# Two-block transformer kernel: the order of the second block's attention units, and where its selection rounds run

## The reference

```
x = x + hybrid_mixer(rms_norm(x))      # dsa and nsa attention, 8 heads each
x = x + memory_xattn(rms_norm(x), mem)
x = x + sq_relu_mlp(rms_norm(x))
```

```
idx_score = sum over heads of relu(qi . ki) * wi, causal
sel       = top 128 keys of idx_score                      # "dsa"
o_dsa     = softmax(qd . kd over sel) . vd
o_cmp     = masked_softmax(qn . kc) . vc                   # 31 compressed keys
o_slc     = softmax(qn . ks over selected blocks) . vs
o_win     = softmax(qn . kw in a window of 512) . vw
o_nsa     = gate0 * o_cmp + gate1 * o_slc + gate2 * o_win
out       = concat(o_dsa, o_nsa) @ w_out
```

## Time and profile before

| | us |
|---|---|
| time, median of 3 runs | 2523.76 (2520.18 to 2527.74) |
| profiled execution, time | 2526.07 |
| profiled execution, span on the core | 2523.9 |
| PE busy in it | 2429.9 (96%) |
| DVE busy | 1228.2 (49%) |
| ACT busy | 930.3 (37%) |
| POOL busy | 1227.3 (49%) |

### The profile page before, as it was taken

One profiled execution on the slowest core, in us unless ns is written; L12 is line 12 of the kernel. 1 busy time (PEld: TensorE's weight loads), 2 busy tenths in 40 slices (PEclk: granted clock), 3 DMA queues, 4 the chain that ended last, 5 costly groups with the idle time before them and its releaser, 6 DMA issues.

```text
span 2523.9 us, 33202 instructions
## 1 busy us (share of the span) xinstructions
PE 2429.9 (96%) x12413; PEld 1945.3 (77%) x12413; DVE 1228.2 (49%) x2251; ACT 930.3 (37%) x1471; POOL 1227.3 (49%) x1594
## 2 busy tenths in 40 slices
PE   7899999999999999999999999998998998999999
PEld 5778777888888778877788878887665667788887
DVE  6885653452335668356333143255688644511211
ACT  5233442432322532244242232244335755423322
POOL 3444445555556645354555555565333432555554
PEclk9999999999999999999999999999898899999999
DMA  4222322332222232222233223233210011222222
GB/s 158 85 81 72 92 67 91 107 105 99 94 98 92 92 101 79 82 84 72 88 100 125 95 90 100 88 105 109 75 63 18 2 38 39 99 93 100 94 99 92
DMA packets 81294, 218.57 MB, mean 87 GB/s; under 512 B 15856, under 2 KB 25456, under 8 KB 80752
## 3 DMA queue, kind: packets, MB, share of 16 engines
q1 hardware_dynamic: 61920, 200.96, 24.3%
q10 hardware_dynamic: 19216, 15.51, 2.2%
HBM read 207.78 MB, written 2.10 MB: 83 GB/s over the span
## 4 chain that ended last, share of the span: by engine, by line
PE 83%; DVE 11%; ACT 2%; issue 2%; ACTq 1%; POOL 1%; DMA 0%; DVEq 0%
PE psG L1007 25%; PE psG L1009 24%; PE psG L1008 24%; PE psT L1184 2%; PE psS L1163 2%; DVE work_b L2048 1%; PE psO L1217 1%; DVE work_m L2048 1%; DVE tmp L2048 1%; ACTq L1700 1%; DVE work_b L2513 1%; PE psS L1094 1%; DVE max L2512 1%; DVE small_work L2048 1%; PE psG L1163 0%
## 5 line engine op out<-in xcount | busy, mean ns | idle before, releaser
L946 POOL TENSOR_TENSOR w_lo<-w_raw,w_hi 128x256 fp32r<-128x256 f32 (+1 forms) x1482 | 1156.2, 810 | 1188.4 <-ACT w_hi L1569 1188.3
L1007 PE MATMUL psG<-h_hi,w_hi 128*128 128x512 f32 x1880 | 751.1, 400 | 12.4 <-POOL w_lo L946 4.1
L1008 PE MATMUL psG<-h_lo,w_hi 128*128 128x512 f32 x1880 | 737.1, 392 | 0.0
L1009 PE MATMUL psG<-h_hi,w_lo 128*128 128x512 f32 x1880 | 736.8, 392 | 0.0
L1569 ACT ACTIVATE w_hi<-w_raw 128x1024 fp32r<-128x1024 f32 (+4 forms) x417 | 404.0, 969 | 501.1 <-PE psG L1009 485.8
L1007 PEld LDWEIGHTS psG<-h_hi,w_hi 128*128 128x128 f32 x1880 | 356.3, 189 | 103.7 <-issue 18.4
L1009 PEld LDWEIGHTS psG<-h_hi,w_lo 128*128 128x128 f32 x1880 | 355.7, 189 | 75.4
L1008 PEld LDWEIGHTS psG<-h_lo,w_hi 128*128 128x128 f32 x1880 | 356.7, 190 | 73.0 <-issue 1.9
L1007 PE MATMUL psG<-m_hi,w_hi 128*128 128x512 f32 x800 | 311.8, 390 | 1.1 <-DVE m_lo L2048 1.1
L1009 PE MATMUL psG<-m_hi,w_lo 128*128 128x512 f32 x800 | 311.5, 389 | 0.0
L1008 PE MATMUL psG<-m_lo,w_hi 128*128 128x512 f32 x800 | 311.4, 389 | 0.0
(11 more groups left out here) (359 smaller groups left out, 2592.5 us busy)
## 6 DMA issues: line engine op xcount, KB each, us to landing
w_raw<-wstream SPq DMA_DIRECT2D x327, 512.0 KB, 3.3
w_raw<-wstream SPq DMA_DIRECT2D x64, 256.0 KB, 2.6
w_raw<-wstream SPq DMA_DIRECT2D x16, 384.0 KB, 3.0
work_b<-work_b ACTq DMA_DIRECT2D x16, 256.0 KB, 3.8
work_b<-cmpw ACTq DMA_DIRECT2D x2, 2048.0 KB, 8.9
x<-xT SPq DMA_DIRECT2D x4, 512.0 KB, 7.9
small_work<-ssmp ACTq DMA_DIRECT2D x8, 256.0 KB, 2.8
outT<-x SPq DMA_DIRECT2D x8, 256.0 KB, 2.0
```

The source lines that it names most:

```text
L946: ins = pool.tensor_tensor(lo[:, c], w[:, c], hi[:, c].bitcast(F32), ALU.subtract)
L1007: pe.matmul(out, whi, hi, start=(k == 0), stop=False)
L1008: pe.matmul(out, whi, lo, start=False, stop=False)
L1009: ins = pe.matmul(out, wlo, hi, start=False, stop=(k == K - 1))
```

## The change

- `SELECT_EACH` becomes a table by product: three rounds in most waves of K = 8, one in waves of K = 1 or 2, two in some, none in the last two (`("uq", 3)` and `("p2", "qn3")`) nor behind them. 23 of the 48 rounds then run in the projections and 25 beside attention. Since the heads of query block 1 are issued only once round 8 of block 2 is chosen, these heads move three waves down.
- `BLOCK2_ORDER` becomes `BLOCK2_PAIRS`. Units of nsa 3 alternate with those of nsa 0, dsa 3 with dsa 0, nsa 2 with nsa 1, dsa 2 with dsa 1. The two `cmp` units of a pair of lists stand side by side. The two lists of a pair use different output banks, and both outputs come at the end of the pair.
- The waits on compressed probabilities follow the new order.
- After the projections PE runs five matmuls of constants (128x256) whose result nobody reads, once the last product's bank is free.
- ACT computes one dummy Exp ahead of attention's first.

```diff
-SELECT_EACH = 3
+SELECT_EACH = {("p2", "kc"): 2, ("kvd",): 1, ("p2", "vs"): 3, ("kd",): 1, ("p2", "vw"): 3, ("uq", 0): 1, ("p2", "qn0"): 3,
+               ("uq", 1): 1, ("p2", "vc"): 2, ("p2", "qn1"): 3, ("uq", 2): 1, ("p2", "qn2"): 2}
...
-BLOCK2_ORDER = [("nsa", 3), ("dsa", 3), ("nsa", 2), ("nsa", 1), ("nsa", 0), ("dsa", 0), ("dsa", 2), ("dsa", 1)]
+BLOCK2_PAIRS = [(("nsa", 3), ("nsa", 0)), (("dsa", 3), ("dsa", 0)), (("nsa", 2), ("nsa", 1)), (("dsa", 2), ("dsa", 1))]
...
-    for kind, b in BLOCK2_ORDER:
-        lists[kind, b] = (units_nsa if kind == "nsa" else units_dsa)(b)
+    block2 = []
+    for large, small in BLOCK2_PAIRS:
+        for kind, b in (large, small):
+            lists[kind, b] = (units_nsa if kind == "nsa" else units_dsa)(b)
+        for two in zip(lists[large], lists[small]):
+            block2 += two
...
+    for key in [key for two in BLOCK2_PAIRS for key in two]:
+        for u in lists[key]:
+            u["group"] = lists[key][-1]["group"]
+    lists["block2"] = block2
...
-            each = SELECT_EACH if s_ < len(PROJECTIONS) else 1 if steps[chosen][1] == 8 else 0
+            each = SELECT_EACH.get(PROJECTIONS[s_], 0) if s_ < len(PROJECTIONS) else 0
...
-                    pe.wait_ge(s_cprob, NB - u["b"])
+                    pe.wait_ge(s_cprob, cmp_units.index(u) + 1)
...
             project(block2_posts)
+            who, count = taken[[key for key in PROJECTIONS if number[key] % GEMM_BANKS == 2][-1]]
+            pe.wait_ge(s_took[who], count)
+            for i in range(5):
+                pe.matmul(psG[:, 2, 0:2 * P], ident, CON[:, 0:2 * P], start=True, stop=True)
             pe.wait_ge(s_p["out"], block2_done["out"])
...
                 if u["kind"] == "cmp":
-                    if u["b"] + 2 < NB:
-                        act.wait_ge(s_pv, units["nsa", u["b"] + 2][-1]["v"] + 1)
+                    for before in cmp_units[:cmp_units.index(u)]:
+                        if before["b"] % 2 == u["b"] % 2:
+                            act.wait_ge(s_pv, units["nsa", before["b"]][-1]["v"] + 1)
...
                 la = ahead(us[0])
+                do(act.activation(stat[:, 3, 11:12], eps, ACT.Exp))
```

5 lines of the change are left out of this document (3 added, 2 removed).

## The result

The changed kernel took 2528.57 us (median of 22 runs, 2526.41 to 2535.28); the kernel before, run beside it, 2526.30 us (22 runs). The ratio is 1.0014, 95% interval 1.0008 to 1.0020: 0.14% slower, within 0.3%. I had predicted 2512.5 us, 0.45% faster, with a range that ended at 2525. The forecast was wrong. It started from 2523.76 us, the median of three runs of the kernel before; with 22 runs that kernel stands at 2526.30. So 2.5 of the 16.1 us between forecast and result lie in the base, and 13.6 in the sum: -11.3 forecast, +2.3 measured.

The account below looks back on a forecast made before the run. DVE's queue with 42 selection rounds was taken to bound the projections, PE attention's long units, latency the short ones. -13.0 + 0.6 + 0.7 + 0.4 = -11.3 us made 2512.5 us (-0.45%), range 2499 to 2525 us.

Parts of the forecast that it names:

- The tail: End of the projections: DVE's last two query steps without rounds ahead or between, 1905.7 in place of 1910.7, -5.0 us.
- T0: Start of attention (its first scores), 1910.76 us before; claimed earlier by 13.0 us, bounds 5 and 19.
- The holes of the projections: PE's other idle time in the projection stretch, about 11 us, two thirds of it to go: -7.5 us.
- the clock: PE's clock in the projection stretch, 0.85 before; less time at 1.2 GHz, counted as 0.5 us saved.
- Attention: All lists of attention, with pairs and 19 more rounds: about 136.5 against 135.90 us, +0.6; bounds 131.5 and 144.
- first two pairs: Start of attention, summed in DVE's order of scores, masks, reciprocals and rounds: 18.9 us.
- lists of 2 and 1: Eight pairs at 4.4, the compressed pair with its rounds 8.9, two outputs 2.9: 47.0 us.
- last lists: End of attention, priced on ACT, with the last chain and two outputs at the end instead of one: 16.8 us.
- The pair of 4.65: A (512, 128) pair in attention, by PE's order and its only pair of transpose banks: 4.65 us, before 5.33.
- The small edits: Around the start of attention: five constant matmuls cost 0.7 us net, the early Exp table load 0.
- Slower: Rival: DVE bounds attention and pairs do not overlap, from a pair time of 5.3 us on; +10, 2534 us; chance 0.10.
- Only the tail pays: Rival: rounds did not hold PE in the projections; -5.0 + 1.7, 2520.5 us, no change; chance 0.16.

Follow-up runs that it names:

- b4: Kernel before, with only the six rounds of its last two projection steps moved beside attention's units 0 to 11; ratio 0.9998 to the kernel before.
- b2: Changed kernel with the same 23 rounds in the projections, but 17 in the first six steps, so block 1's heads come earlier; ratio 1.0005 to the kernel before.
- b1: Changed kernel without the 25 rounds beside attention (selection unfinished, only for timing); ratio 0.9993 to the kernel before.
- d1: Changed kernel with PE issuing a unit's transposes ahead of the scores of the unit four places on; ratio 1.0000 to the kernel before.
- c4: Changed kernel with 33 rounds in the projections, 15 beside attention at units 4 to 23, only blocks 3 and 0 alternating; ratio 0.9994 to the kernel before.
- a3: Changed kernel with only the lists of blocks 3 and 0 alternating, the others list by list; ratio 0.9996 to the kernel before.
- c1: Changed kernel without the five constant matmuls; ratio 1.0029 to the kernel before.
- c2: Changed kernel without the early Exp; ratio 1.0016 to the kernel before.

## Why the prediction was wrong

**The tail, -5.0.** Right in kind, too large: 3.9 us (b4). I gave DVE 5.6 us from the root to T0, and it takes 6.85.

**The holes of the projections, -7.5, and the clock, -0.5.** The size was near: with the heads in their old place the whole comes to 10.2 us to T0 (b2), of which 3.9 are the tail, so 6.3 for the 8.0. The change got 6.6 - 3.9 = 2.7. What failed is the step from rounds to holes. I counted the rounds that go, and not what else the table orders: a block's first round is the leave for the next block's heads. These moved three steps down, onto the windows of the second compression, and opened the hole of 4.12 us and a cold compression: 3.5 us net given back (b2). The order of instructions of the changed kernel showed that move; I read it only at the places where rounds stood.

**Attention, +0.6.** By its lines, in the order of the prediction's sum: first two pairs 18.9, measured 22.98; seven pairs 32.6, measured 34.27; dsa lists 20.9, measured 20.38; lists of 2 and 1 47.0, measured 47.64; last lists 16.8, measured 19.22. Sum 136.2 against 144.49. Three terms failed.
- The first two pairs, by 4.1 us. DVE's order was the right account, but my list of it was short. It took the second pair of 512-key masks at 0.8 us instead of 1.6, and put the end of these masks 17.6 us after T0 where DVE reached it after 19.2. And it ended with a round of DVE (1.25 us), where the copy also needs PE's scores and transposes, 1.78 + 1.97 us. At full clock those would take 2.1 (1.06 + 1.03): PE waits for DVE in small pieces here, and the stretch has a clock of 0.70. The rounds there cost 2.8 us (b1).
- The last lists, by 2.4. I took ACT's 4.24 us a pair plus a chain; PE's 4.48 is the bound, and lists of like lengths gain nothing from alternation.
- The pair of 4.65, measured 4.88: the mechanism was the one I gave, and d1 confirms it; the size was off by 0.23, 1.7 us in seven pairs.

The dsa lists and the lists of blocks 2 and 1 were priced within 0.7 us. So I had the loss of the latter, 7.3 us against the 39.7 of the serial order, in my own sum, and let it be covered by a gain in the first lists of 7.3 us (18.9 + 32.6 against 39.0 + 19.8 = 58.8 for the same units before) that is 1.6 us: 57.2, rounds included. The sentence that failed is "That slack is what the alternation can win": it holds for the pairs in the clear (4.88 against 5.33), and the first two pairs, with both compressed units and the rounds in DVE's queue, take most of it back. That 47.0 came so near for blocks 2 and 1 is in part luck: I priced two compressed units side by side, and of the 7.9 us lost there 3.5 are the rounds (b1), some 4 come in the serial order too (c4), and the pairing itself is worth 0.4 to 1.3 (b1 against c4, a3).

**The small edits, +0.7 and 0.** Wrong in sign: about -3.9 for the matmuls (c1), and 0 to -3 for the Exp (c2). They are in the measured attention, which without the matmuls would be 148.5.

**The waits on buffers, +0.4.** Not seen apart; no run took them out alone.

**The rivals.** None came out whole. "Slower" had the right mechanism in part: masks, rounds and neighbouring compressed units in one queue, and the compressed pairs stood open. But it priced it over the pair time (from 5.3 us on), which stayed below 4.9. "Only the tail pays" was near for T0 (5.0 us, measured 6.6), for the wrong reason. The range was too narrow because T0 and attention were not allowed to fail together: with the lower bound of T0 (-5) and the upper of attention (144, so +8.1) my own sum gives +4.2 us, and the measured parts are -6.6 and +8.5, attention just beyond its bound.
